# Eight expert weight chunks get tiles of their own, and the later ones shift through the twelve slots

## The reference

```python
def hierarchical_moe(h, w_rg, b_rg, w_re, b_re, w1, w3, w2):
    ...
    g_gate, g_idx = lax.top_k(softmax(t @ w_rg + b_rg), 1)       # one group of four
    e_logits = ... of that group
    e_w, e_idx = lax.top_k(softmax(e_logits), TOP_K)             # two experts of eight
    weight = g_gate * e_w / sum(e_w)
    combine = jnp.sum(one_hot(expert_id, N_EXPERTS) * weight[..., None], axis=1)

    def expert_block(args):
        tk, c = args
        hid = silu(einsum('td,edf->tef', tk, w1)) * einsum('td,edf->tef', tk, w3)
        return einsum('tef,efd->td', hid * c[:, :, None], w2)

# first_block
h2 = rmsnorm(x, norm2_g)
x = x + hierarchical_moe(h2, w_rg, b_rg, w_re, b_re, w1, w3, w2)
# second_block: x goes through hybrid_layer (norm, projections, attention, convolution, feed-forward)
```

## Time and profile before

| what | value |
|---|---|
| three runs | 1800.24, 1805.28, 1809.12 us, median 1805.28 |
| profiled execution | 1804.82 us, its span 1803.2 us |
| mean granted TensorE clock | 0.99 of 2.4 GHz |
| TensorE busy | 1754.9 us, 97% of the span |
| VectorE, ScalarE, GpSimd busy | 879.2, 579.7, 752.1 us |
| DMA | 268.44 MB, mean 149 GB/s |
| `ring` requests | 324 of 512 KB, median 3.6 us to landing |
| `more` requests | 48 of 1024 KB, median 9.4 us to landing |

### The profile page before, as it was taken

One profiled execution on the slowest core, in us unless ns is written; L12 is line 12 of the kernel. 1 busy time (PEld: TensorE's weight loads), 2 busy tenths in 40 slices (PEclk: granted clock), 3 DMA queues, 4 the chain that ended last, 5 costly groups with the idle time before them and its releaser, 6 DMA issues.

```text
span 1803.2 us, 22923 instructions
## 1 busy us (share of the span) xinstructions
PE 1754.9 (97%) x8545; PEld 1308.3 (73%) x8545; DVE 879.2 (49%) x1322; ACT 579.7 (32%) x1084; POOL 752.1 (42%) x623
## 2 busy tenths in 40 slices
PE   9999999998999989999999899999999999999999
PEld 6888877776887434443688676776788788888887
DVE  4221786658663234332551679997467442112211
ACT  3223444544232111111231345555462322212220
POOL 4454434334441000000341458887735544545442
PEclk9999999998999999999999899999999999999999
DMA  6222222224344899999721422221354222322321
GB/s 232 98 83 93 92 89 85 74 88 146 111 146 152 310 383 371 394 409 385 296 99 56 147 91 71 71 73 64 98 200 152 94 82 96 103 94 94 95 93 47
DMA packets 82936, 268.44 MB, mean 149 GB/s; under 512 B 8337, under 2 KB 9361, under 8 KB 82833
## 3 DMA queue, kind: packets, MB, share of 16 engines
q1 hardware_dynamic: 64608, 230.31, 36.3%
q10 hardware_dynamic: 15920, 28.32, 4.5%
q0 software_dynamic: 2304, 8.39, 1.3%
HBM read 249.16 MB, written 17.83 MB: 148 GB/s over the span
## 4 chain that ended last, share of the span: by engine, by line
PE 85%; DVE 10%; DMA 3%; issue 1%; ACT 1%; POOL 0%; SPq 0%; ACTq 0%; DVEq 0%; POOLq 0%
PE psum L618 82%; DMA more<-stream 3%; DVE area L2129 2%; DVE area L2188 1%; DVE negm L2169 1%; DVE gh L2202 1%; PE psum L1016 1%; PE psum L748 1%; DVE area L2701 1%; DVE area_r L2072 0%; PE psum L1392 0%; DVE gh L2196 0%; DVE den L2198 0%; DVE area_r L2071 0%; DVE area L2289 0%
## 5 line engine op out<-in xcount | busy, mean ns | idle before, releaser
L618 PE MATMUL psum<-area_r,ring_hi 128*128 128x512 f32 x3104 | 974.7, 395 | 4.5 <-DVE area_r L2072 1.4
L495 POOL TENSOR_TENSOR ring_lo<-ring,ring_hi 128x512 fp32r<-128x512 f32 x420 | 564.4, 1366 | 787.2 <-ACT ring_hi L1557 783.0
L618 PEld LDWEIGHTS psum<-area_r,ring_hi 128*128 128x128 f32 x3104 | 577.5, 189 | 131.5 <-issue 14.2
L618 PE MATMUL psum<-area_r,ring_lo 128*128 128x512 f32 x1552 | 606.9, 391 | 0.0
L1557 ACT ACTIVATE ring_hi<-ring 128x1024 fp32r<-128x1024 f32 x210 | 221.6, 1059 | 550.5 <-PE psum L618 515.0
L618 PEld LDWEIGHTS psum<-area_r,ring_lo 128*128 128x128 f32 x1552 | 292.3, 188 | 62.3
L1557 ACT ACTIVATE area<-psum 128x512 f32<-128x512 f32 (+3 forms) x252 | 124.0, 518 | 239.1 <-PE psum L748 73.7
L618 PE MATMUL psum<-ring,area 128*64 128x512 f32 (+1 forms) x480 | 134.0, 601 | 2.8 <-DMA ring<-stream 1.9
L618 PE MATMUL psum<-area 128*64 128x128 f32 (+7 forms) x864 | 113.6, 340 | 7.5 <-DVE negm L2178 5.7
L2072 DVE TENSOR_TENSOR area_r<-area,area_r 128x512 fp32r<-128x512 f32 x90 | 104.5, 1162 | 3.1
L551 POOL DMA_INDIRECT area<-tokens,idx x16 | 15.2, 951 | 205.9 <-DVE idx L2434 162.0
(11 more groups left out here) (246 smaller groups left out, 1598.3 us busy)
## 6 DMA issues: line engine op xcount, KB each, us to landing
ring<-stream SPq DMA_DIRECT2D x324, 512.0 KB, 3.6
more<-stream SPq DMA_DIRECT2D x48, 1024.0 KB, 9.4
gates<-root ACTq DMA_DIRECT2D x24, 256.0 KB, 2.0
area<-gates SPq DMA_DIRECT2D x24, 256.0 KB, 5.6
gates<-area ACTq DMA_DIRECT2D x20, 256.0 KB, 4.4
area<-gates ACTq DMA_DIRECT2D x20, 256.0 KB, 5.0
area<-xT SPq DMA_DIRECT2D x8, 256.0 KB, 4.5
area<-xT ACTq DMA_DIRECT2D x8, 256.0 KB, 3.5
```

The source lines that it names most:

```text
L495: ins = nc.gpsimd.tensor_tensor(ring_lo[:, c % RS, n], ring[:, c % R, n], ring_hi[:, c % RS, n].bitcast(F32), ALU.subtract)
L618: return nc.tensor.matmul(out, lhsT, rhs, start=first, stop=last)
```

## The change

The expert chunks 12 to 19 are loaded early to eight places of their own, `early[0..3]` on tiles 48 to 55 and `early[4..7]` on tiles 32 to 39, each with one request. The first four are asked for once `lg_mm` is reached, ahead of the last two `mkv` chunks and the pairs of `more1` and `more2`; the other four behind the second expert chunk, once `xt_t` is 8. They land on the semaphores `x_rest` and `params_in`. All chunks from 20 on take the slot that chunk minus 8 would have had. After the early eight, 184 are left: fifteen turns of twelve (`TURNS`) and four, which go to `more1` and `more2`. The dense form reads its normed tokens from tiles 40 to 47 (`HD`) so that 48 to 55 stay free, and takes its first and last group out of the loop.

```diff
+EARLY = 8
+TURNS = (MOE1 - MOE0 - EARLY) // RM
...
+def moe_place(i):
+    if RM <= i < RM + EARLY:
+        return "early", i - RM, 0
+    j = i if i < RM else i - EARLY
+    if j >= TURNS * RM:
+        return "more", j % RM + 2, TURNS + 1
+    return ("ring" if j % RM < R else "more"), j % RM - (0 if j % RM < R else R), j // RM + 1
...
+        early = [area[:, 48 + 2 * n:50 + 2 * n, :] for n in range(4)] + [area[:, 32 + 2 * n:34 + 2 * n, :] for n in range(4)]
...
             sp.wait_ge(weights_used, MK0)
             load_two(MOE0 + R, 0)
+            def load_early(n, landing):
+                sp.dma_start(early[n], stream[bass.ds(MOE0 + RM + n, 1)].rearrange("a p n -> p (a n)")).then_inc(landing, 16)
+            sp.wait_ge(S("lg_mm"), 1)
+            for n in range(4):
+                load_early(n, S("x_rest"))
             for c in range(MK0 + R, MOE0):
                 sp.wait_ge(weights_used, c - R + 1)
                 load(c, c % R)
...
             for c in range(MOE0, MOE0 + R):
                 sp.wait_ge(weights_used, c - R + 1)
                 load(c, c % R)
-            with sp.Fori(0, (MOE1 - MOE0) // RM - 1) as t:
+                if c == MOE0 + 1:
+                    sp.wait_ge(S("xt_t"), KD)
+                    for n in range(4, EARLY):
+                        load_early(n, params_in)
+            for i in range(R):
+                sp.wait_ge(weights_used, MOE0 + i + 1)
+                load(MOE0 + EARLY + RM + i, (MOE0 + i) % R)
+            for x in range(3):
+                sp.wait_ge(weights_used, MOE0 + R + 2 * x + 2)
+                load_two(MOE0 + EARLY + RM + R + 2 * x, x)
+            with sp.Fori(0, TURNS - 2) as t:
                 for i in range(R):
-                    sp.wait_ge(weights_used, t * RM + (MOE0 + i + 1))
-                    load(t * RM + (MOE0 + RM + i), (MOE0 + i) % R)
+                    sp.wait_ge(weights_used, t * RM + (MOE0 + EARLY + RM + i + 1))
+                    load(t * RM + (MOE0 + EARLY + 2 * RM + i), (MOE0 + i) % R)
                 for x in range(3):
...
-            for c in range(MOE1, MOE1 + R):
-                sp.wait_ge(weights_used, c - RM + 1)
-                load(c, c % R)
+            for x in (1, 2):
+                sp.wait_ge(weights_used, MOE0 + EARLY + (TURNS - 1) * RM + R + 2 * x + 2)
+                load_two(MOE0 + EARLY + TURNS * RM + 2 * (x - 1), x)
+            for i in range(R):
+                sp.wait_ge(weights_used, MOE0 + EARLY + (TURNS - 1) * RM + i + 1)
+                load(MOE1 + i, (MOE1 + i) % R)
...
-            def arrived(c, turns):
+            def arrived(where, i, count, turns=0):
+                if where == "early":
+                    if i < 4:
+                        pe.wait_ge(S("x_rest"), 8 * KD + 16 * 4)
+                    else:
+                        pe.wait_ge(params_in, 32 + 16 * 4)
+                    return early[i]
```

More of the change, by code:

```diff
@@ L229, in block_program @@
             (high_at + 4 * 512 * (NT + PAIRS), area_at + 2048 * XT, area_at + 2048 * (XT + 4)))]
+        early = [area[:, 48 + 2 * n:50 + 2 * n, :] for n in range(4)] + [area[:, 32 + 2 * n:34 + 2 * n, :] for n in range(4)]
+        early = [t.rearrange("p a b -> p (a b)") for t in early]
         LAST2 = (0, 7)
@@ L1193, in dense @@
                 pe.wait_ge(S("rt_out"), 2)
-                mm(psum[:, 5, :], ones[:], tile(SQ1), True, False)
-                mm(psum[:, 5, :], ones[:], tile(SQ1 + KD - 1), False, True).then_inc(S("fb_sum"), 1)
+                for t in range(NT):
+                    ins = mm(psum[:, 5, P * t:P * t + P], den[:, t:t + 1].to_broadcast([P, P]), ident[:], True, True)
+                ins.then_inc(S("fb_sum"), 1)
                 for t in range(NT):
@@ L1198, in dense, with dense_group @@
                 ins.then_inc(S("fb_sum"), 1)
-                pe.wait_ge(S("fb_root"), 2 + KD + 1)
-                with pe.Fori(0, GROUPS) as g:
+                pe.wait_ge(S("fb_root"), 1 + KD + 1)
+                def dense_group(g, of):
                     for step, p in SEQ:
@@ L1207, in dense @@
                                 for ex in range(2):
-                                    c = C0["moe"] + GC[step, p] + 2 * kp + ex
-                                    w13 = arrived(c, g * (16 * CPG // RM))
+                                    c = GC[step, p] + 2 * kp + ex
+                                    w13 = of(c)
                                     for f in range(FE):
@@ L1223, in dense @@
                                 for x in range(4):
-                                    c = C0["moe"] + GC[step, p] + x
+                                    c = GC[step, p] + x
                                     if m == 0:
-                                        w2s[x] = arrived(c, g * (16 * CPG // RM))
+                                        w2s[x] = of(c)
                                     f, ex = divmod(x, 2)
@@ L1233, in dense, with of_group @@
                                     ins.then_inc(S("fb_y"), 1)
-                nx_sums()
-            def arrived(c, turns):
-                i = (c - MOE0) % RM
-                if i < R:
-                    pe.wait_ge(loads[(MOE0 + i) % R], 16 * landed(c) + turns)
+                def of_group(g):
+                    return lambda c: arrived(*moe_place(CPG * g + c))
+                dense_group(0, of_group(0))
+                with pe.Fori(1, GROUPS - 1) as g:
+                    dense_group(g, lambda c: arrived(*moe_place(CPG + c), (g - 1) * (16 * CPG // RM)))
+                dense_group(GROUPS - 1, of_group(GROUPS - 1))
+                nx_sums()
+            def arrived(where, i, count, turns=0):
[5 more added lines that the diff above has]
+                    return early[i]
+                if where == "ring":
+                    pe.wait_ge(loads[(MOE0 + i) % R], 16 * ((MOE0 + i) // R + count) + turns)
                     return ring[:, (MOE0 + i) % R, :]
-                x, half = divmod(i - R, 2)
-                pe.wait_ge(S(f"more{x}"), 16 * ((c - MOE0) // RM + 1) + turns)
+                x, half = divmod(i, 2)
+                pe.wait_ge(S(f"more{x}"), 16 * count + turns)
                 return ring2[x][:, half, :]
@@ L2546, in dense @@
                 dve.wait_ge(S("fb_root"), 1)
-                V.reciprocal(root[:, 0, :], root[:, 0, :]).then_inc(S("fb_root"), 1)
-                dve.wait_ge(S("fb_root"), 2)
+                dve.wait_ge(mem_in, 16 + 64)
                 for k in range(KD):
-                    V.scalar_tensor_tensor(out=tile(HF + k), in0=tile(X + k), scalar=par("norm2", k), in1=root[:, 0, :],
+                    V.scalar_tensor_tensor(out=tile(HD + k), in0=tile(X + k), scalar=par("norm2", k), in1=root[:, 0, :],
                                            op0=ALU.mult, op1=ALU.mult).then_inc(S("fb_root"), 1)
```

19 lines of the change are left out of this document (8 added, 11 removed).

## The result

The changed kernel takes 1807.99 us (median of 20 runs, 1803.98 to 1812.12), the kernel before 1804.45 us (20 runs; one of them took 5455.31 us and has no part in the ratio). The ratio is 1.0023, with a 95% interval of [1.0016, 1.0031]: 2.9 to 5.6 us slower. I had forecast 1805.0 us and no change. The size is inside my range and inside the 9 us that I had called no change, but so many runs tell it apart from none, and the sign is slower. The profiled execution of the changed kernel took 1805.46 us (span 1803.8), 2.5 us under its own median.

What follows compares the result with a forecast made beforehand. The prediction took TensorE, 82% of the chain of waits through one matmul helper, to bound the kernel, with expert weights arriving late in group 0. Sum: 1804.82 - 8.0 + 0.1 + 8.1 + 0 = 1805.0 us; range 1797 to 1811.

Steps and rivals of the forecast that it cites:

- The first group gains: Group 0, expert chunks 28 to 31: 4.81 us of TensorE waits and the low clock behind them go, 8.0 us gained.
- rival 3: Group 0's wait is not bought off: gain 0, loss of 8.1 at the stage's end, 1812.9 us; chance 0.05.
- The lead is not kept: Groups 1 to 3: the eight-chunk lead cannot reach them, their 3.5 us of waits stay; 0, bounds -2.5 and +2.5.
- Rival 4: Groups 1 to 3: the slot shift lengthens each wait by 1.3 us, half clock follows, 1818.8 us; chance 0.05.
- The early loads cost room before the stage: Before the stage: eight early loads delay chunks 2 to 5, 0 to 1 us of wait, taken as 0.1.
- The end of the stage loses: Stage end: late last pair and next-stage chunks delay the last scatter; 8.1 us lost, bounds 1.0 and 12.7.
- The pair's wait: Stage end: TensorE waits 1.0 us for the last expert pair, chunks 190 and 191.
- ScalarE's wait: Stage end: ScalarE waits about 12 us for the next stage's first chunk, 6.17 us before.
- the one for `yt_lo`: Stage end: TensorE stands 3.7 us before the last scatter, waiting for `yt_lo`.
- The second wait of 0.7: Last scatter, eight matmuls in: TensorE waits 0.7 us for `yt_lo` of expert pair 3.
- the clock's 2.6: Last scatter: half clock behind the long wait costs 2.6 or 2.7 us.
- Rivals 1 and 2: Stage end: tail stays at full clock, 1802.3 us, chance 0.20; or tail is nearly hidden, 1797.8 us, chance 0.12.

Runs made afterwards that it cites:

- the two repeats: The kernel before and the changed kernel, each run once more unaltered with a second profiled execution: 1803.32 us and 1810.25 us.
- the repeat: The changed kernel run once more, unaltered, against the kernel before: 1810.25 us, ratio 1.0034.
- the last version: Changed kernel with early loads behind the token store and ring chunks, slots turned eight places so the last four chunks find free ones, against the kernel before: 1797.72 us, 0.9963.

## Why the prediction was wrong, step by step

*The first group gains: 8.0.* Right: 7.7 us between the two traces, 7.3 between the two repeats. The waits are gone and the clock is 1.00. No wait for gathered rows took its place, and rival 3 is out. The DMA pause that I had argued is there (0.75 in 624:644, was 1.03).

*The lead is not kept: 0.* Right within its bounds: the windows of 660:748 have TensorE at 36.00 and 51.23 (36.00 and 50.95 before), and the waits at 849.86 and 853.07 (1.9 us) stand where 854.35 and 856.95 did (2.0). The stretch is 1.4 us shorter, but the kernel before differs by as much between two executions (214.6 and 216.0). Rival 4 is out.

*The early loads cost room before the stage: 0.1.* This is the step that failed: TensorE waits 4.1 us, the head is 4.4 us longer in the traces, and 4 to 6 us in medians (1.0023 or 1.0034 to 1.0001, and 1.0000 to 0.9972). I had written that the memory weights, the pairs and the token rows "are wanted by TensorE long after they come; a few us late they are still early", and took the 14% free in 572:590 as room. The first half is true, since four extra loads there cost nothing. The room is not. It lies in front of the store (0.69 in 572:578), and what fills it holds the store back, so that a hole opens behind it (0.71 in 584:590; 0.63 to 0.76 in the other traces with these loads); moved behind the store, the loads leave it empty (0.46). In either order hardly more was carried by 590 (at most 0.7 of 2.1 MB).

A second fault lies beside it: I had not looked up when these four chunks landed. Chunk 5 was in at 609.4 and wanted at 610.8, a margin of 1.4 us. The room that could be used up to there was 2.8 us in 590:604 and 43% of 5.4 us in 604:609.4, 2.3 us. My sum, done for chunk 5 and with the 2.5 us of 572:590 still in it, is 10.2 - 2.5 - 2.8 - 2.3 = 2.6 us late, and a wait of 1.2 us. Without the 2.5 us it is 5.1 us late and a wait of 3.7 us. So the room that was none is the larger part. Both are estimates. The traces agree: counted from the table load, chunk 5 landed 5.6 us later than before (615.8 against 609.4, less the 0.8), 5.3 in the repeat, and less the margin this is 4.2 and 3.9 us, where the waits are 4.1 and 3.9. With only the second four moved it landed 0.6 us later, inside the margin.

How did the loads hold the store back? It was asked at 573.77 and landed at 585.7. Its packets are those of the DMA queue q10 (ScalarE's), and the first moved 3.5 to 4 us after the request (4.5 to 5 with only the second four moved); in the kernel before and wherever no load stood in front, it was under 1 us. Then the two queues in 579:584 of the changed kernel (packets, MB, share of the 16 engines' time; q1 is SP's):

```profile
q1 hardware_dynamic: 360, 1.29, 65.0%
q10 hardware_dynamic: 365, 0.75, 38.3%
```

A rule of the Trainium skill (DMA: Bandwidth & Descriptors, Queues, rings and completion order) has each DMA engine take turns between the queues, packet by packet. The trace agrees: 365 packets of the store to 360 of SP's loads, 366 to 365 in the repeat, 359 to 358 with four unused loads. But the store's packets are the smaller ones, 0.75 MB to 1.29. So it got 0.15 MB per us, of 0.41. Why its first packet moved so late, no run shows.

*The end of the stage loses: 8.1.* Right in mechanism, a little large: 6.2. The pair's wait was 1.12 (I had 1.0), ScalarE's wait 12.19 (12), the one for `yt_lo` 4.13 (3.7). The second wait of 0.7 did not come, and of the clock's 2.6 about 1.5 show. Behind the 4.13 us wait the clock was 0.50 for 3.4 us; where it was 1.12 us it stayed at 1.00. I had misread one row for this: behind the 1.88 us wait of the earlier trace rows the eight matmuls took 1.94 us and the clock in 624:644 was 1.00, so only the 2.93 us wait of group 0 drew the half clock. By the Trainium skill (TensorE: Matmul & The Clock Gate, HAM oscillation) work behind a DMA wait starts on the slow clock. The traces agree only in part: not for waits of about 1 us, and for waits of 1.9 to 3.4 us in some executions and not in others. Rivals 1 and 2 are out.

In the profiled executions then: -7.7 - 1.4 + 4.4 + 6.2 = +1.5 at the next stage's first matmul, and with the 0.8 us from before the stage the 2.3 between 897.13 and 899.45. The medians have +3.5, and +6.4 in the repeat. A part may be the clock behind the head's wait: it stayed at 1.00 in the two profiles of the unaltered change, but in all three experiments that leave the head as it is (the order of the next stage's requests, ScalarE's order, the dummy matmuls) it fell there, to 0.91 over 604:624. Their heads took 46.9, 47.6 and 46.2 us, with 46.5 and 46.2 where it did not fall, so that is 1.4 us at most. Where the rest lies is not shown.

## What to carry to other kernels

A share of idle DMA in a window is room only if something can be put there without delaying what the idle time stands in front of. Ask which request ends the pause, and what waits for it. Count extra bytes against the next deadline in the queue, each free microsecond once. And where chunks are left over at the end of a ring, turn the slots so that the end falls on free ones: requests are in order, and the next stage's are behind them.

## What the runs showed of the hardware

I had not expected a 1 MB store to take 11.9 us and not 4.8 because 2 MB of loads stood in another engine's queue (12.3 us where four loads were all that was added, 4.8 again where they were moved behind it). Its first packet came late, and from then on it got half of the packets, but little more than a third of the bytes. And a wait of TensorE of 2 to 3 us was followed by the half clock in some executions and not in others: 2.94 us at 612.78 in the changed kernel was not; 2.06 us at 873.67 was, with the next stage's requests first, and 2.06 us at 845.88 in the last version was not.
